# First input transfer cut to one K tile, and the zero products' memset moved to the head of VectorE

## The reference

```
for i in range(DEPTH):
    h = rms_norm(x, norm_mix_g[i])
    x = x + (moba_mixer(h, a_w_qkv, ...) if i % 2 == 0 else retention_mixer(h, r_w_in, ...))
    x = x + sqrelu_mlp(rms_norm(x, norm_mlp_g[i]), mlp_w1[i], mlp_w2[i])
```

## Time and profile before

| | us |
|---|---|
| three runs | 666.35, 666.40, 667.74 |
| median | 666.4 |
| profiled execution, first to last instruction (span) | 665.3 |
| median less span (start and end of an execution, outside the span) | 1.1 |
| TensorE busy | 659.8 (99%) |
| VectorE, ScalarE, GpSimd busy | 423.6 (64%), 332.1 (50%), 26.8 (4%) |

### The profile page before, as it was taken

The page is one execution under the profiler, slowest core; times in us unless marked ns, Lnnn a source line. Parts: engine busy times, 40 slices in busy tenths (PEclk is TensorE's granted clock), DMA queues, the critical chain, the costliest instruction groups (busy, mean ns, idle before and its releaser), DMA issues.

```text
span 665.3 us, 8894 instructions
## 1 busy us (share of the span) xinstructions
PE 659.8 (99%) x3296; PEld 557.4 (84%) x3296; DVE 423.6 (64%) x469; ACT 332.1 (50%) x435; POOL 26.8 (4%) x29
## 2 busy tenths in 40 slices
PE   8999999999999999999999999999999999999998
PEld 7888888888888888888888888888888888888887
DVE  6898666877776454459875555654478777744541
ACT  6877655655554334364446455454365555533320
POOL 0163000000000000000000000000000000000000
PEclk9999999999999999999999999999999999999999
DMA  9965456766555555535665455356637665556600
GB/s 316 388 225 186 134 163 226 224 198 190 195 191 203 190 190 188 191 127 191 193 210 167 144 172 188 126 169 185 206 113 221 190 184 189 191 197 206 195 1 32
DMA packets 82125, 123.00 MB, mean 185 GB/s; under 512 B 2352, under 2 KB 43824, under 8 KB 82096
## 3 DMA queue, kind: packets, MB, share of 16 engines
q1 hardware_dynamic: 81808, 121.28, 56.7%
q0 software_dynamic: 288, 1.31, 0.5%
HBM read 121.54 MB, written 1.05 MB: 184 GB/s over the span
## 4 chain that ended last, share of the span: by engine, by line
PE 99%; DVE 0%; issue 0%; DVEq 0%
PE acc L585 22%; PE acc L489 19%; PE acc L491 19%; PE acc L490 19%; PE acc L588 11%; PE scr L599 1%; PE acc L533 1%; PE acc L612 1%; PE acc L536 1%; PE scr L491 1%; PE scr L489 1%; PE scr L490 1%; PE acc L542 1%; PE scr L625 1%; PE scr L718 1%; PE scr L636 1%
## 5 line engine op out<-in xcount | busy, mean ns | idle before, releaser
L1004 DVE TENSOR_TENSOR lo<-raw,hi 128x2048 fp32r<-128x2048 f32 x108 | 247.3, 2290 | 115.9 <-ACT hi L773 115.8
L773 ACT ACTIVATE hi<-raw 128x2048 fp32r<-128x2048 f32 x108 | 207.0, 1918 | 129.9 <-PE acc L491 127.8
L585 PE MATMUL acc<-h_both,hi 128*128 128x512 f32 x640 | 223.1, 395 | 0.0
L588 PE MATMUL acc<-h_both,lo 128*128 128x256 f32 x640 | 177.8, 278 | 0.0
L585 PEld LDWEIGHTS acc<-h_both,hi 128*128 128x128 f32 x640 | 120.1, 188 | 28.1
L588 PEld LDWEIGHTS acc<-h_both,lo 128*128 128x128 f32 x640 | 120.3, 188 | 0.0
L489 PE MATMUL acc<-hi,aT_hi 128*128 128x512 f32 x252 | 98.1, 389 | 0.0
L491 PE MATMUL acc<-hi,aT_lo 128*128 128x512 f32 x252 | 98.1, 389 | 0.0
L490 PE MATMUL acc<-lo,aT_hi 128*128 128x512 f32 x252 | 98.0, 389 | 0.0
L489 PE MATMUL acc<-hi,h_both 128*128 128x512 f32 x208 | 83.6, 402 | 0.0
L491 PE MATMUL acc<-hi,h_both 128*128 128x512 f32 x208 | 81.2, 391 | 0.0
(11 more groups left out here) (130 smaller groups left out, 585.9 us busy)
## 6 DMA issues: line engine op xcount, KB each, us to landing
raw<-in_mlp_w SPq DMA_DIRECT2D x64, 1024.0 KB, 5.4
raw<-in_r_w_in SPq DMA_DIRECT2D x24, 1024.0 KB, 5.1
raw<-in_a_w_qkv SPq DMA_DIRECT2D x8, 1024.0 KB, 9.9
raw<-in_r_w_out SPq DMA_DIRECT2D x8, 1024.0 KB, 4.9
raw<-in_a_w_qkv SPq DMA_DIRECT2D x16, 256.0 KB, 6.5
raw<-in_a_w_o SPq DMA_DIRECT2D x4, 1024.0 KB, 5.1
x<-in_x SPq DMA_DIRECT2D x1, 1024.0 KB, 12.2
decay_sb<-in_decay POOLq DMA_DIRECT2D x1, 768.0 KB, 6.6
```

The costliest lines, as they stand in the source:

```text
L585: nc.tensor.matmul(bank, feat_view(hi, s)[:, kt, o * P:(o + 1) * P], h_both[:, kt, :, :].rearrange("p b t -> p (b t)"), start=kt == 0, sto ...
L588: m = nc.tensor.matmul(bank[:, 0:SEQ], feat_view(lo, s)[:, kt, o * P:(o + 1) * P], hT_hi[:, kt, :], start=False, stop=kt == KD - 1)
L773: nc.scalar.activation(hi[:, s, :], raw[:, s, :], ACT.Copy).then_inc(hi_ready, 1)
L1004: nc.vector.tensor_tensor(lo[:, s, :], raw[:, s, :], hi[:, s, :].bitcast(F32), ALU.subtract).then_inc(lo_ready, 1)
```

## The change

The first input transfer carries the gains and K tile 0 alone (144 KB in place of 272 KB). K tile 1 has a transfer of its own (128 KB), issued after the first weight piece, and the second weight piece follows it. The other two input pieces hold the same K tiles as before. The memset of `sT` goes to the head of VectorE's program, ahead of the five increments.

```diff
-XT_PIECES = [range(0, 2), range(2, 4), range(4, KD)]
+XT_PIECES = [range(0, 1), range(1, 2), range(2, 4), range(4, KD)]
...
             load_xT(0)
-            load_parts(0, [0, 1])
+            load_parts(0, [0])
             load_xT(1)
+            load_parts(0, [1])
+            load_xT(2)
             load_parts(0, [2, 3])
-            load_xT(2)
+            load_xT(3)
             load_parts(1)
...
         @block.vector
         def _(dve):
+            nc.vector.memset(sT[:], 0.0).then_inc(zeros_ready, 1)
             dve.sem_inc(lo_ready, RING)
             dve.sem_inc(hT_ready, 4)
             dve.sem_inc(acc_free, 4)
...
-            nc.vector.memset(sT[:], 0.0).then_inc(zeros_ready, 1)
             for c in range(2):
```

## The result

The change made the kernel slower. In 20 runs each, the kernel before has a median of 667.43 us (665.97 to 669.50) and the changed one 668.76 us (666.61 to 670.47); the ratio is 1.0018, 95% interval 1.0009 to 1.0026, so about 1.2 us slower (0.6 to 1.7). The three runs from which the prediction started were low for their kernel: the same code has a median 1.0 us above them. The two profiles of the changed kernel agree on where the time goes.

A forecast was written before the change was run, and what follows sets the result against it. TensorE was taken as the bound, busy 659.8 of 665.3 us. Of a head gain of 0.15 to 0.45 us, 0.14 was kept: 666.4 - 0.14 = 666.26, given as 666.3 us; range 665.6 to 667.1.

The forecast's parts named there:

- the memset: Head of VectorE: sT's memset, then the zero products, start 0.6 us earlier (bounds 0 to 0.61), at no price.
- the first weight piece: Early transfers: with 128 KB less ahead of it, it lands 0.3 us earlier (bounds 0 to 0.5).
- the head gain: TensorE at the start: 0.45 us gained if the clock's rise follows the zero products, 0.15 if not.
- I take 0.1 us for every later landing: SyncE's queue behind the added transfer: each later piece lands 0.1 us later (bounds 0 and 0.45).
- The bound of one issue slot: SyncE's queue: the added DMA delays later issues about 0.45 us, taken as the most a landing could slip.
- The slack at the third piece: TensorE's weight load at 8.56: slack 0.31 us, of which 0.2 can be kept with the landing 0.1 later.
- The chain from chunk 4: ScalarE and VectorE, 21.32 to 61 us: limits TensorE's gain to 0.24 us idle time less 0.1 delay, 0.14.
- Rival B: Chunk 4: the extra transfer costs more than 0.24 us there, up to 0.2 slower, 666.6 us; chance 0.2.
- Rival C: After the zero products: TensorE's pause makes the clock rise late, 1.5 us slower, 667.9 us; chance 0.1.
- The start value: Whole kernel before: median of three runs 666.4 us, 1.1 us above the profiled span, taken as unchanged.
- The scatter that was allowed: Whole run time: 0.1% scatter of the measured median, included in the forecast's range.

The follow-up runs named there:

- e1: The memset's part of the diff alone, against the kernel before; ratio 1.0001 (0.9992 to 1.0010).
- e5: Kernel before with the 16 KB load of the gains moved from behind the mask to behind chunk 1's pieces; ratio 1.0011 (1.0002 to 1.0020).
- e13: Kernel before with eight increments of an unused semaphore on SyncE behind chunk 1, no transfer added; ratio 0.9992 (0.9980 to 1.0004).
- e12: Kernel before with eight increments of an unused semaphore on SyncE between first and second weight piece, a 0.4 us pause; ratio 1.0006 (0.9995 to 1.0017).
- e6: Changed kernel with the input transfers of K tiles 0 and 1 issued by ScalarE; ratio to the kernel before 1.0006 (0.9996 to 1.0017).
- e10: Second run of e6, K tiles 0 and 1 issued by ScalarE; ratio to the kernel before 1.0005 (0.9994 to 1.0016).
- e3: Kernel before with the 16 KB load of the gains issued early, between first and second weight piece; ratio 1.0014 (1.0004 to 1.0023).
- e4: Changed kernel with K tile 1's input transfer issued by ScalarE before its table load; ratio to the kernel before 1.0003 (0.9993 to 1.0014).
- e9: Second run of e4, K tile 1 issued by ScalarE; ratio to the kernel before 1.0001 (0.9989 to 1.0013).
- e0: The kernel before once more, unchanged, for the scatter of its landings; ratio 0.9992 (0.9981 to 1.0003).
- e14: Second run of e3, the 16 KB load issued early; ratio to the kernel before 1.0002 (0.9993 to 1.0011).
- e11: Kernel before with two small loads moved early, the gains (16 KB) and the identity (64 KB); ratio 1.0023 (1.0014 to 1.0032).
- e8: The changed kernel once more; ratio to the kernel before 1.0009 (1.0000 to 1.0018).

## Why the prediction was wrong

It forecast 0.14 us faster, in effect no change, and the kernel got slower: by 1.2 and 0.6 us in two comparisons of runs, by 0.7 to 0.8 us at the mark.

- **Right: the memset, at a smaller size.** 0.46 us earlier instead of 0.6; in all kernels with the memset at the head it starts at 0.90, not at 0.75. It costs nothing that e1 could show.
- **Right in number, not shown in cause: the first weight piece** 0.31 us earlier (0.3 forecast), first product at 5.03 (5.04). Seven kernels with the uncut first transfer have the piece at 4.19 to 4.25 as well, and most of them their first product at 5.02. The profile before had simply drawn a late landing (4.57), so the agreement is in part luck.
- **Right: the head gain.** TensorE is 0.31 us ahead at the first product and 0.44 to 0.58 us until the end of K tile 1 (0.15 to 0.45 forecast, the higher end if the clock rises earlier, and it did: the pairs are 0.46 apart from 5.89 on).
- **Wrong, and this decides: "I take 0.1 us for every later landing".** The bounds were 0 and 0.45. Measured: 0.9 us at the third piece and 1.15 us at chunk 4 in this profile, 0.88 us at chunk 4 over five profiles against five, 0.5 us where it was smallest; all of them outside the bounds. The step that failed is the reading of the earlier trace rows: from the median of sixteen pieces (6.5 us from issue to landing) it took it that transfers wait for one another and not for their issue. That is so further on, where e5 and e13 show no price. But the added issue stands at 1.67 us, where the piece ahead of it lands 3.3 us after its own issue, and there a later issue is a later landing. In the windows up to 9 us the profiles show 263 to 377 GB/s and not 395, and what is missed then is not made up, since from 9 us on every kernel runs at 390 to 395. The bound of one issue slot (0.45) was also too low, if only by 0.05 us where the price was smallest: e12's pure delay passes on at about its own size, an added issue costs as much or up to twice that.
- **The slack at the third piece was larger than worked out.** 0.31 us was counted to the weight load at 8.56, but a weight load runs ahead of its matmuls (8.79) when it may. The load came at 9.14, the matmuls at 9.17 (the chain from ScalarE's end at 9.03 fits), 0.38 us late: 0.89 of delay less a slack of 0.51.
- **The chain from chunk 4 was the right mechanism, with too little slack.** It holds as described (the load at 61.50 starts 0.05 us after VectorE's 61.45), and it sets the mark in both profiles of the changed kernel. The 0.24 us of listed idle time stood for a slack of 0.37, because listed ends of ScalarE reach past the next start when nothing is waited for: in the changed kernel the instruction ahead of the copy is listed to 26.65 and the copy starts at 26.53. So the mark is 1.15 - 0.36 = 0.79 us late. TensorE alone, by its own lag at K tile 3 and 4, would have been 0.5 to 0.7 us late.
- **Rival B was the right mechanism at a wrong size**: 0.2 us and a chance of 0.2, where 0.7 belonged. Its point of decision (0.24 us at chunk 4) was exceeded.
- **Rival C did not happen** in this kernel's profiles (pairs 0.46 apart by 6 us in both), against the fear that the pause after the zero products does it. What the Trainium skill says of it (TensorE: Matmul & The Clock Gate, Part 1), that the point of change differs from run to run, is borne out: two profiles of one kernel reach the full pace at 5.5 us (e6) and 10.1 us (e10).
- **The start value.** Median of three, 666.4, where 20 runs give 667.4. The prediction took 1.1 us for the time outside the span, from a span and a median of different executions; wherever an execution has both on record, the difference is 1.7 to 2.2 us. With it, the profile's 665.3 would have pointed to 667.3. The range of 665.6 to 667.1 would have missed an unchanged kernel too. The scatter that was allowed (0.1%) was too small; the 20 runs of the kernel before span 3.5 us.

What stays open: whether a transfer by SyncE costs more than the time of its issue in the first microseconds (up to 0.4 us more on the mean), and if so, why. e3 shows that neither size nor row length is needed for the loss, and e4 that an issue by another engine does not bring it.

## What to carry to other kernels

At the start of a program, count issues and not bytes: there a further transfer on the same queue pushed back everything behind it by its issue time or more (0.5 to 0.9 us here), while 5 us later it showed no price. Judge a queue as full only by the transfers at the place in question, not by a median over all: issues that take longer than the first ones (0.6 against 0.47 us here) are a sign of it. If an early piece must be split, letting an idle engine issue the added part avoids the loss (e4, e9). Before crediting a change with an early landing, look at how that landing scatters in unchanged kernels. And do not judge a gain of 0.3 us by run times that scatter by 3.

## What the runs showed of the hardware

**Two paces of the same loop.** The profile of e0 is longer than that of before by 1.0 us though the code is the same. 0.8 of it come from two stretches in which TensorE does not wait. First and last start of the 128 x 256 matmuls of the first MLP product (line 588: count, duration in ns min/median/max, first to last start in us), in before and in e0:

```profile
L588 PE MATMUL acc<-h_both,lo x256: 274/277/280, 113.2 to 201.6; 128*128 128x256 f32 x128
```

```profile
L588 PE MATMUL acc<-h_both,lo x256: 277/281/284, 113.3 to 203.4; 128*128 128x256 f32 x128
```

88.4 against 90.1 us for the same 256 steps, 1.9% slower in pace and 277 against 281 ns in the median duration, at a granted clock of 1.00. The retention projection has the same two paces (line 588, 128 steps), here before, then the changed kernel:

```profile
L588 PE MATMUL acc<-h_both,lo x128: 277/281/284, 291.4 to 336.3; 128*128 128x256 f32 x128
```

```profile
L590 PE MATMUL acc<-h_both,lo x128: 274/277/280, 293.9 to 337.9; 128*128 128x256 f32 x128
```

44.9 against 44.0 us. Every one of the 18 profiles has one or the other in each stretch (eight have the slow pace in the first, eight in the second). Between before and the changed kernel all the rest of the program after 60 us is the same within 0.1 us. The two stretches can account for 1.7 and 0.9 us of the 3.5 by which runs scatter. They also account for the spans of before and after: the changed kernel had the slow pace in the first stretch and the fast one in the second, 1.7 - 0.9 = 0.8 us net, beside the 0.79 at the mark. I don't know what sets the pace, nor whether the start can influence it; the slow pace of the first stretch appears in e0 and e1 as well as in both profiles of the changed kernel.

**The clock's rise.** The granted clock reads 1.00 throughout, so the distance between pairs shows the level: 0.85 us at 1.2 GHz, 0.46 at 2.4. With the zero products from 1.80 us on, the first pair at 2.4 GHz starts between 5.8 (e14) and 7.7 us (e11); with them from 1.33 on, mostly at 5 to 7 us and once at 10.1 (e10). The kernel's time depends on it only where the pieces do not already hold TensorE: e8 reaches 2.4 GHz by 5.3 us and still has its mark at 61.62, e5 after 7 us and has it at 60.92.
